# The rotary half turn by quarters of 32 partitions on VectorE and GpSimd, in place of a matrix product on TensorE

## The reference, cut to what matters

```python
def apply_rope(x, cos, sin):
    x1, x2 = jnp.split(xf, 2, axis=-1)          # 32 + 32 of a head's 64 channels
    return concatenate([x1 * c - x2 * s, x2 * c + x1 * s], axis=-1)

def diff_attention(...):                        # kind A
    q = apply_rope(...); k = apply_rope(...)
    p = softmax(where(causal, q @ k.T * scale, -inf))
    wts = p[:, :, 0] - lam * p[:, :, 1]
    o = rms_norm_2(wts @ v, subln_g) * (1.0 - lam_init)
```

## Time and profile before

| what | value |
|---|---|
| median of 3 runs | 2439.07 us (2437.29 to 2443.3) |
| the profiled execution, its own time | 2438.7 us |
| its span in the trace | 2436.2 us |
| TensorE busy | 2377.8 us, 98% of the span |
| VectorE busy | 1729.0 us, 71% |
| ScalarE busy | 1192.0 us, 49% |
| GpSimd busy | 90.1 us, 4% |
| from 1200 to 1320 us (first stage A) | PE 117.62, DVE 86.45 us busy |
| from 1835 to 1920 us (stage C) | PE 76.19, DVE 58.44 us busy |
| from 2120 to 2245 us (second stage A) | PE 122.62, DVE 93.05 us busy |

### The profile page before, as it was taken

How to read it: one execution, slowest core, us unless ns; L and a number is a source line. 1 busy time by engine, 2 the same in 40 slices (tenths; PEclk the granted TensorE clock), 3 DMA queues, 4 the chain that set the end, 5 groups by cost and what they waited for, 6 DMA issues and landing times.

```text
span 2436.2 us, 46453 instructions
## 1 busy us (share of the span) xinstructions
PE 2377.8 (98%) x19243; PEld 2289.4 (94%) x19243; DVE 1729.0 (71%) x2263; ACT 1192.0 (49%) x1488; POOL 90.1 (4%) x166
## 2 busy tenths in 40 slices
PE   6999999999999999999999999999998999999998
PEld 6999989999999989999988999899997999988998
DVE  7888788777777867655677666776667656677665
ACT  5335865434433755433556435654345533556433
POOL 1110000000010000000000000100000000000000
PEclk9999999999999999999999999999999999999999
DMA  9896465887788533455433554435542355442552
GB/s 352 313 321 244 156 227 188 283 287 258 272 286 277 182 139 107 174 187 189 160 131 126 207 189 156 146 114 207 189 172 87 124 205 181 149 154 105 207 196 96
DMA packets 75560, 471.60 MB, mean 194 GB/s; under 512 B 8632, under 2 KB 9144, under 8 KB 26808
## 3 DMA queue, kind: packets, MB, share of 16 engines
q1 hardware_dynamic: 56288, 400.79, 45.7%
q0 software_dynamic: 18432, 67.12, 8.0%
q10 hardware_dynamic: 728, 2.14, 0.3%
HBM read 468.96 MB, written 1.05 MB: 193 GB/s over the span
## 4 chain that ended last, share of the span: by engine, by line
PE 86%; DVE 7%; ACT 3%; issue 2%; DMA 1%; SPq 0%; ACTq 0%; DVEq 0%
PE bank L2194 25%; PE bank L2196 25%; PE bank L2195 25%; DVE w_lo L1245 2%; PE bank L2205 1%; PE bank L2200 1%; PE bank L2201 1%; ACT w_hi L617 1%; DMA ARENA<-in_first 1%; PE bank L2383 1%; PE bank L2415 0%; DVE ada_wbuf L1383 0%; DVE ARENA L1438 0%; DMA ada_wbuf<-in_ada 0%; PE bank L2565 0%
## 5 line engine op out<-in xcount | busy, mean ns | idle before, releaser
L1245 DVE TENSOR_TENSOR w_lo<-w_raw,w_hi 128x2048 fp32r<-128x2048 f32 x371 | 849.8, 2292 | 323.0 <-ACT w_hi L617 322.0
L617 ACT ACTIVATE w_hi<-w_raw 128x2048 fp32r<-128x2048 f32 x371 | 708.5, 1913 | 524.2 <-PE bank L2196 513.5
L2194 PE MATMUL bank<-h_hi,w_hi 128*128 128x256 f32 x3376 | 950.0, 281 | 4.1 <-DVE w_lo L1245 3.1
L2196 PE MATMUL bank<-h_hi,w_lo 128*128 128x256 f32 x3376 | 939.7, 278 | 0.0
L2195 PE MATMUL bank<-h_lo,w_hi 128*128 128x256 f32 x3376 | 939.6, 278 | 0.0
L2194 PEld LDWEIGHTS bank<-h_hi,w_hi 128*128 128x128 f32 x3376 | 633.8, 188 | 11.3 <-issue 6.8
L2195 PEld LDWEIGHTS bank<-h_lo,w_hi 128*128 128x128 f32 x3376 | 633.6, 188 | 3.6 <-issue 3.3
L2196 PEld LDWEIGHTS bank<-h_hi,w_lo 128*128 128x128 f32 x3376 | 634.2, 188 | 0.0
L2194 PE MATMUL bank<-d_hi,w_hi 128*128 128x256 f32 x1920 | 539.9, 281 | 3.2 <-DVE d_lo L1611 3.1
L2196 PE MATMUL bank<-d_hi,w_lo 128*128 128x256 f32 x1920 | 535.6, 279 | 0.0
L2195 PE MATMUL bank<-d_lo,w_hi 128*128 128x256 f32 x1920 | 535.4, 279 | 0.0
(11 more groups left out here) (392 smaller groups left out, 2277.1 us busy)
## 6 DMA issues: line engine op xcount, KB each, us to landing
w_raw<-in_ws SPq DMA_DIRECT2D x371, 1024.0 KB, 4.8
ada_wbuf<-in_ada POOLq DMA_DIRECT2D x128, 512.0 KB, 5.1
ARENA<-in_first SPq DMA_DIRECT2D x8, 1024.0 KB, 19.5
work<-in_x SPq DMA_DIRECT2D x1, 1024.0 KB, 11.0
ARENA<-in_wax ACTq DMA_DIRECT2D x1, 1024.0 KB, 4.7
out_y<-ARENA SPq DMA_DIRECT2D x4, 256.0 KB, 2.1
ARENA<-in_wg ACTq DMA_DIRECT2D x1, 768.0 KB
c_rows<-in_c SPq DMA_DIRECT2D x1, 512.0 KB, 4.7
```

The lines of the kernel that those rows point to most:

```text
L617: act.activation(w_hi[:, slot, :], w_raw[:, slot, :], ACT.Copy).then_inc(hi_ready, 1)
L1245: dve.tensor_tensor(w_lo[:, s, :], w_raw[:, s, :], w_hi[:, s, :].bitcast(F32), ALU.subtract).then_inc(lo_ready, 1)
L2194: pe.matmul(o, whi, xhi, start=start, stop=False, skip_group_check=True)
L2196: return pe.matmul(o, wlo, xhi, start=False, stop=stop, skip_group_check=True)
```

## The change

The matrix `turn` and the product on TensorE go. `rot_b` is written by four operations of 32 partitions each, which read `raw` and `sin_r` at rows 32q to 32q+31 and write `rot_b` at the neighbouring 32 rows: quarters 0 and 1 on VectorE, 2 and 3 on GpSimd. The sign moves into the sine table, through the scale of the activation that makes it. VectorE still waits for `turned`, which GpSimd now gives after quarter 3; GpSimd waits for `sin_scaled` (once a stage), `proj_ready` and `roped` of the rotation before. In the product of weights and values in A a wait on `roped` goes.

```diff
+        def turned_quarter(eng, kind, k, q, nt):
+            rows, other = slice(32 * q, 32 * q + 32), slice(32 * (q ^ 1), 32 * (q ^ 1) + 32)
+            return eng.tensor_tensor(rot_b[other, 0:nt, :], raw_part(kind, k)[rows, 0:nt, :],
+                                     sin_r[rows, :].unsqueeze(1).broadcast_to([32, nt, T]), ALU.mult)
...
+            for quarter in range(4):
+                link(pool.memset(half_sign[32 * quarter:32 * quarter + 32, :], -1.0 if quarter % 2 else 1.0))
-            keep(halves[:, :, 0:32], ALU.not_equal, -1.0, -32, [[-64, 2], [-1, 32]], 1)
-            keep(halves[:, :, 32:64], ALU.not_equal, 1.0, 0, [[-64, 2], [-1, 32]], 1)
...
+            def turn_halves(st, k):
+                kind = st["key"][0]
+                piece, nt = ROT_PIECE[kind][k], 1 if kind == "C" and k == 0 else 2
+                if k == 0:
+                    pool.wait_ge(sin_scaled, st["turns"] + 1)
+                pool.wait_ge(proj_ready, st["evac"] + piece + 1)
+                if st["rots"] + k:
+                    pool.wait_ge(roped, st["rots"] + k)
+                for q in (2, 3):
+                    ins = turned_quarter(pool, kind, k, q, nt)
+                ins.then_inc(turned, 1)
...
-                        act.activation(t[:, :], rope_w[2 + 2 * k], ACT.Sin).then_inc(rope_ready, 1)
+                        act.activation(t[:, :], rope_w[2 + 2 * k], ACT.Sin,
+                                       scale=half_sign[:, 0:1] if k == 0 else 1.0).then_inc(rope_ready, 1)
...
-                    link(dve.tensor_tensor(sin_r, sin_t[:, :], rstd[:, :], ALU.mult))
                     chained()
+                    dve.tensor_tensor(sin_r, sin_t[:, :], rstd[:, :], ALU.mult).then_inc(sin_scaled, 1)
+                    dve.wait_ge(sin_scaled, st["turns"] + 1)
...
                 link(dve.tensor_tensor(rot_a[:, 0:nt, :], raw_part(kind, k)[:, 0:nt, :], cosb, ALU.mult))
+                for q in (0, 1):
+                    link(turned_quarter(dve, kind, k, q, nt))
                 dve.wait_ge(turned, st["rots"] + k + 1)
-                m = MISC[:, 0:nt * T].rearrange("p (t n) -> p t n", t=nt)
-                link(dve.tensor_tensor(rot_b[:, 0:nt, :], m, sinb, ALU.mult))
                 chained()
...
-            def turn_pair(st, k, units):
-                pe.wait_ge(proj_ready, st["evac"] + piece + 1)
-                if k == 0:
-                    pe.wait_ge(r_col_ready, st["cols"] + 1)
...
-                m = MISC[:, 0:nt * T].rearrange("p (t n) -> p t n", t=nt)
-                pe.matmul(m, turn[:, :], raw_part(kind, k)[:, 0:nt, :], start=True, stop=True).then_inc(turned, 1)
...
                 if kind == "A":
-                    pe.wait_ge(roped, st["rots"] + rots)
```

More of the change, by code:

```diff
@@ L139, in __init__ @@
                                    cols=sum(s[0] in "ABC" for s in stages[:k]),
+                                   turns=sum(s[0] in "AC" for s in stages[:k]),
                                    scales=8 * sum(s[0] == "B" for s in stages[:k])))
@@ L220, in build @@
         later = sb("later", [P, P])
-        turn = sb("turn", [P, P])
+        half_sign = sb("half_sign", [P, 1])
         cos_t = sb("cos_t", [P, T])
@@ L380, in build @@
         turned = sem("turned")
+        sin_scaled = sem("sin_scaled")
         roped = sem("roped")
@@ L557, in _ @@
                 link(pool.memset(t[:, :], 1.0))
-            for t in (turn, a_mask, c_mask):
+            for t in (a_mask, c_mask):
                 link(pool.memset(t[:, :], 0.0))
-            halves = turn[:, :].rearrange("p (h c) -> p h c", h=2)
+            for quarter in range(4):
+                link(pool.memset(half_sign[32 * quarter:32 * quarter + 32, :], -1.0 if quarter % 2 else 1.0))
             def keep(view, op, fill, base, pattern, multiplier):
@@ L599, in _ @@
                             pool.tensor_tensor(sp, sp, both, ALU.mult).then_inc(spm_ready, 1)
+                elif st["key"][0] in "AC":
+                    for k in range(ROTS[st["key"][0]]):
+                        turn_halves(st, k)
         @block.scalar
@@ L1635, in rotate @@
                 cosb = cos_r.unsqueeze(1).broadcast_to([P, nt, T])
-                sinb = sin_r.unsqueeze(1).broadcast_to([P, nt, T])
                 link(dve.tensor_tensor(rot_a[:, 0:nt, :], raw_part(kind, k)[:, 0:nt, :], cosb, ALU.mult))
+                for q in (0, 1):
+                    link(turned_quarter(dve, kind, k, q, nt))
                 dve.wait_ge(turned, st["rots"] + k + 1)
-                m = MISC[:, 0:nt * T].rearrange("p (t n) -> p t n", t=nt)
-                link(dve.tensor_tensor(rot_b[:, 0:nt, :], m, sinb, ALU.mult))
                 chained()
@@ L2367, in attention_input @@
                     value_columns(st)
-            def turn_pair(st, k, units):
-                kind = st["key"][0]
-                piece, nt = ROT_PIECE[kind][k], 1 if kind == "C" and k == 0 else 2
-                pe.wait_ge(proj_ready, st["evac"] + piece + 1)
-                if k == 0:
-                    pe.wait_ge(r_col_ready, st["cols"] + 1)
[L2376 to L2381, removed]
-                m = MISC[:, 0:nt * T].rearrange("p (t n) -> p t n", t=nt)
-                pe.matmul(m, turn[:, :], raw_part(kind, k)[:, 0:nt, :], start=True, stop=True).then_inc(turned, 1)
             def scores(st, u):
@@ L2538, in attention @@
                     elif step == "rot":
-                        turn_pair(st, k, outs if kind == "A" else 0)
                         rots += 1
```

## The result

The changed kernel takes 2461.07 us, the median of six runs (2457.3 to 2469.41); the kernel before took 2441.19 in the same sessions (2436.54 to 2451.95). The ratio is 1.0068, with a 95% interval of 1.004 to 1.0095: slower, by 10 to 23 us. I had forecast slower, by 9 us, at 2448. The direction was right and the size was not: by the ratio it is 16.6 us, by the two medians 19.9, and the median lies above the 2454 of the forecast's own case and 1 us above the 2460 at which the stated range ended.

The account below looks back on a forecast made before the run. TensorE, busy 98% of the span, was taken as the bound, with VectorE setting the pace after the change. Two A stages at +2 and C at +5 gave +9 us on 2438.7: 2448, range 2432 to 2460.

Parts of the forecast that it names:

- the forecast's own case: Whole kernel: one quarter exposed in A's periods, both in some; 2443 to 2454 us, chance 0.48.
- Exclusion: All rotations: VectorE's operations on SBUF stand still while GpSimd multiplies; only one quarter fits beneath the maxima, 1.26 us.
- the first rival: A and C: no quarter exposed, loop 7.91 us, -13 us, 2426; chance 0.20 together with cheap quarters.
- Price of a quarter on GpSimd: Each GpSimd 32x512 product: 1.16 us taken, ends 0.61 and 1.86.
- The start of A: First scores of A: second rotation ready at 1223.4, TensorE waits 2.0 us, 0.4 of 2.5 us removed are left.
- The loops of A: A's periods: VectorE 7.91 us, 9.07 with one exposed quarter, 10.23 with both; TensorE alone 7.94.
- The stage from the loops: Each A: +0.2 us with one exposed quarter, +2 with a third of 5.8 more; range -6 to +6.
- C: Stage C: late first scores +2.7, half clock +1.8, dearer rotations and exposed quarter behind; +5 us, range 0 to +8.
- Sum: Whole kernel: two A at +2 and C at +5 give +9 us on 2438.7, so 2448.
- The dear rival: A and C: both quarters exposed, each A +6, C +7.5, +19.5 us, 2458; chance 0.20.

Follow-up runs that it names:

- e3: Kernel before, its turn still on TensorE, plus GpSimd multiplying two 32x512 pieces of unrelated data at each rotation, which nobody waits for; 2446.34 us.
- e1: Changed kernel with GpSimd's two quarters covering only 16 of 256 columns of each tile, all waits kept; 2437.48 us.
- e2: Changed kernel with all four quarters of each rotation on VectorE and none on GpSimd; 2466.49 us.
- the second traces: Both kernels run again word for word for another trace; single executions of 2447.17 us (changed) and 2452.77 us (before).

## Why the prediction was right in direction and wrong in size

- *Exclusion:* right. The earlier trace rows had shown one direction; e3 shows it with data that nobody needs. That e1 puts A at 119.2 also shows that the first rival (no quarter exposed) would have come true in A if quarters were free.
- *Price of a quarter on GpSimd:* 1.29 us where nothing holds it, 1.16 taken. Small: 0.13.
- *The start of A:* the first scores at 1224.36, with everything 0.7 later from the opening on; 1223.4 forecast. The wait there was 2.1, forecast 2.0. Right.
- *The loops of A:* from the second maxima to the seventh the mean is (1280.84 - 1233.70) / 5 = 9.43 us, forecast 9.07 + 0.39 = 9.46. So near is in part luck: by e1 VectorE's own work is 8.01 and not 7.91, and 1.42 of GpSimd's comes on top, forecast 1.55. Nor does it come as a third of a quarter in each loop: the gaps alternate, 11.03, 8.00, 11.10, 8.01, 9.00. Where a pair falls into the normalising it is exposed whole, and the rotation behind it finds its quarters done.
- *The stage from the loops:* **the step that failed in A.** "With one exposed quarter A takes +0.2 us" was read off at T4, where TensorE's slack of 3.6 us is just used up; with the third of both quarters exposed it gave +2. That part held: T4 comes at 1278.96, and less the 0.7 of the opening that is 2.5 us late. What was missed is that VectorE's own slack there is smaller. N4 ends 5.7 us later (1278.64 against 1273.05 - 0.84 = 1272.21, less 0.7), and behind it VectorE had only 0.84 + 0.60 = 1.4 us idle up to the maxima of S6. So these come 4.2 later. ScalarE's exponentials wait for them, its `w_hi` and its copies of the values (L864) stand behind these, and W4 waits for the copies. First the kernel before, then the changed one:

```profile
1273.05 2.29 DVE L1245 TENSOR_TENSOR w_lo<-w_raw,w_hi 128x2048 fp32r<-128x2048 f32 x1 [0.84 <-ACT w_hi L617]
1275.95 1.15 DVE L1708 TENSOR_REDUCE ARENA<-bank 128x1 f32<-128x256 f32 x4 [0.60 <-PE bank L2420]
1284.29 0.67 PE L2461 MATMUL bank<-ARENA 128*128 128x256 f32 x2 [0.40 <-ACT ARENA L840]
```

```profile
1278.64 2.28 DVE L1269 TENSOR_TENSOR w_lo<-w_raw,w_hi 128x2048 fp32r<-128x2048 f32 x1
1278.96 0.49 PE L2492 MATMUL bank<-ident,ARENA 128*128 128x128 f32 x3
1280.84 1.14 DVE L1732 TENSOR_REDUCE ARENA<-bank 128x1 f32<-128x256 f32 x4
1289.18 0.67 PE L2468 MATMUL bank<-ARENA 128*128 128x256 f32 x2 [1.92 <-ACT ARENA L864]
```

  W4 is 4.9 later, 4.2 without the opening; the stage ends +4.0 in this trace and +3.0 in the second, where one quarter less lay bare. A1 has +4.9: its opening is the same (first maxima 15.07 us behind its start, 15.05 in A0), 4.4 of it stand at the maxima of S7, and 0.5 come behind them, which stays open. So A was mis-sized: 8.4 for both, 4 forecast.
- *C:* the same mechanisms, each too small. The second maxima came 4.1 later, 3.6 forecast, of which +2.6 (2.7) at the first scores and the rest of the half clock. **What was short is the part behind them:** 3.0 us, where I had 1.2 + 1.2 - 0.5 = 1.9. VectorE has no idle time through these rotations, so what is added to it counts in full: two rotations at +0.89 and not 0.61, and 1.8 us of exposed quarters and not 1.2 (operations on four columns that take 0.73, 0.33 and 1.25 us where 0.16 stood), less the wait of 0.5. e1, with nearly no quarters, keeps C at +2.9; e2, with two operations more in each rotation, has 106.1. C +7.5, +5 forecast.
- *Sum:* 9 forecast; 15.9 in these stages. The 0.9 of B and the FFNs' two paces were in no term, and the FFNs alone can move a single execution by as much as the whole effect, as the second traces show.
- *The dear rival* (both quarters exposed in each period) gave 2458, nearer in total, but for another reason: a mean of 1.1 quarters lay bare (1.42 / 1.29), not two.

## What to carry to other kernels

Work taken from the busiest engine is worth what the next engine in that stage has left: here about 1.5 us in a period of 8.8, and the change laid 0.9 for the dearer rotation and 1.4 of GpSimd's time on it. Ask of a helper engine whether it shuts out the one that you want to spare; GpSimd on SBUF beside a busy VectorE cost in A as much as VectorE doing the work, while ScalarE's copies cost nothing that A's length shows, as long as they do not stand ahead of something that is waited for. When an engine comes late, compare it with each thing that hangs on it up to the end of the stage, and go by the one with the least slack: here the maxima with 1.4 us, not the transposes with 3.6.

## What the runs showed that I had not expected

Each of the last four FFNs runs at one of two paces, 16.32 or 16.96 us a chunk, 6.2 us apart over the stage, and the same code takes now one, now the other. VectorE's product once a chunk, in the kernel before, first and second trace, and windows of 110 us in the same FFN:

```profile
1457.32 0.68 DVE L1551 TENSOR_TENSOR hid<-bank,rstd 128x512 f32<-128x512 f32 x1
1473.64 0.68 DVE L1551 TENSOR_TENSOR hid<-bank,rstd 128x512 f32<-128x512 f32 x1
```

```profile
1446.84 0.69 DVE L1551 TENSOR_TENSOR hid<-bank,rstd 128x512 f32<-128x512 f32 x1
1463.80 0.69 DVE L1551 TENSOR_TENSOR hid<-bank,rstd 128x512 f32<-128x512 f32 x1
```

```profile
1360.00:1470.00 110.00, 110.00 (x973) 110.00 (x973) 67.05 (x55) 41.92 (x28) 0.00 (x0) 1.00 0.54 195
```

```profile
1360.00:1470.00 110.00, 110.00 (x937) 110.00 (x936) 66.53 (x54) 40.11 (x26) 0.00 (x0) 1.00 0.51 182
```

The profile shows no pause of TensorE and a granted clock of 1.00 in both; it does 973 matmuls in one and 937 in the other, 3.7% fewer, on the same form of instruction. The scatter of single runs of one kernel, 2430 to 2459 for the kernel before over all sessions, is of the size that such steps give; that they make it up is not shown. What picks the pace stays open. For this kernel the lesson is that a span compared with a span says less than stages compared with stages.
